# Two layer norms of a decoder layer: GpSimd's share moved to VectorE, the last sums taken by TensorE, and weight splits placed inside the first norm

## The reference, cut to what matters

```
def merge_and_ffn(x, oa, ob, ga, gb, w_oa, w_ob, w_out, ln1_g, ln1_b, w_ffn_in, w_ffn_out, ln2_g, ln2_b):
    pa = oa @ w_oa
    pb = ob @ w_ob
    mix = (sigmoid(ga) * pa + sigmoid(gb) * pb) @ w_out
    h = layer_norm(ALPHA * x + mix, ln1_g, ln1_b)
    gate, up = split(h @ w_ffn_in, 2)
    f = (silu(gate) * up) @ w_ffn_out
    return layer_norm(ALPHA * h + f, ln2_g, ln2_b)

def layer_norm(x, g, b):
    mu = mean(x); var = mean((x - mu) ** 2)
    return (x - mu) * rsqrt(var + 1e-5) * g + b
```

## Time and profile before

| | us |
|---|---|
| median of 3 runs (lowest to highest) | 1821.79 (1819.96 to 1823.74) |
| span of the profiled execution | 1823.3 |
| PE busy in the span | 1747.2 (96%) |
| DVE busy | 995.4 (55%) |
| ACT busy | 725.3 (40%) |
| POOL busy | 156.4 (9%) |

### The profile page before, as it was taken

How to read it: one execution, slowest core, us unless ns; L and a number is a source line. 1 busy time by engine, 2 the same in 40 slices (tenths; PEclk the granted TensorE clock), 3 DMA queues, 4 the chain that set the end, 5 groups by cost and what they waited for, 6 DMA issues and landing times.

```text
span 1823.3 us, 32494 instructions
## 1 busy us (share of the span) xinstructions
PE 1747.2 (96%) x12451; PEld 1660.6 (91%) x12451; DVE 995.4 (55%) x1389; ACT 725.3 (40%) x1054; POOL 156.4 (9%) x257
## 2 busy tenths in 40 slices
PE   8999999998999998999959999999999999999995
PEld 7999999766989896999959999999999999999995
DVE  4457667554377575666664444444444444444546
ACT  4343443353433232334344544443333333333333
POOL 1012222323010100000050000000000000000001
PEclk9999999897999998999979999999999999999997
DMA  6579999668688887677837878876775555556541
GB/s 217 155 267 315 324 321 342 164 180 256 223 301 298 306 290 233 220 228 252 254 128 237 256 246 265 250 230 213 259 224 165 167 161 161 165 167 200 163 155 52
DMA packets 204717, 410.75 MB, mean 225 GB/s; under 512 B 12220, under 2 KB 105686, under 8 KB 200416
## 3 DMA queue, kind: packets, MB, share of 16 engines
q1 hardware_dynamic: 178384, 254.41, 43.7%
q10 hardware_dynamic: 7488, 91.33, 15.0%
q0 software_dynamic: 18768, 63.94, 10.8%
HBM read 403.47 MB, written 94.92 MB: 273 GB/s over the span
## 4 chain that ended last, share of the span: by engine, by line
PE 77%; DVE 8%; DMA 7%; issue 4%; ACT 2%; POOL 1%; DVEq 0%; SPq 0%; ACTq 0%
PE bank L1289 74%; DMA VST<-in_cache_b_dram 3%; PE bank L1292 3%; DMA raw<-in_w_in_dram 3%; DVE wlo L898 1%; DVE PV L1091 1%; DVE PV L1094 1%; POOL U L572 1%; ACT L859 1%; DVE U L1205 1%; DVE U L1195 1%; DVE VST L1082 1%; ACT whi L615 0%; DMA xs_s<-in_x_sample_dram 0%; DVE VST L1085 0%
## 5 line engine op out<-in xcount | busy, mean ns | idle before, releaser
L898 DVE TENSOR_TENSOR wlo<-raw,whi 128x1024 fp32r<-128x1024 f32 x473 | 576.1, 1226 | 646.9 <-ACT whi L615 646.3
L615 ACT ACTIVATE whi<-raw 128x1024 fp32r<-128x1024 f32 x473 | 498.2, 1060 | 837.6 <-PE bank L1289 611.0
L1289 PE MATMUL bank<-X1H,whi 128*128 128x288 f32 x1408 | 420.1, 298 | 17.6 <-DVE X1L L1212 11.7
L1289 PE MATMUL bank<-X1L,whi 128*128 128x288 f32 x1408 | 417.4, 296 | 0.0
L1289 PE MATMUL bank<-X1H,wlo 128*128 128x288 f32 x1408 | 415.8, 295 | 0.0
L1289 PE MATMUL bank<-XH,whi 128*128 128x288 f32 x1248 | 375.1, 301 | 0.7 <-issue 0.5
L1289 PE MATMUL bank<-XL,whi 128*128 128x288 f32 x1248 | 369.9, 296 | 0.0
L1289 PE MATMUL bank<-XH,wlo 128*128 128x288 f32 x1248 | 368.6, 295 | 0.0
L1289 PEld LDWEIGHTS bank<-X1H,whi 128*128 128x128 f32 x1408 | 265.7, 189 | 21.5 <-issue 16.8
L1289 PEld LDWEIGHTS bank<-X1H,wlo 128*128 128x128 f32 x1408 | 267.0, 190 | 0.0
L1289 PEld LDWEIGHTS bank<-X1L,whi 128*128 128x128 f32 x1408 | 266.1, 189 | 0.0
(11 more groups left out here) (234 smaller groups left out, 1789.7 us busy)
## 6 DMA issues: line engine op xcount, KB each, us to landing
raw<-in_w_ffn_in_dram SPq DMA_DIRECT2D x176, 512.0 KB, 3.6
raw<-in_w_in_dram SPq DMA_DIRECT2D x156, 512.0 KB, 6.0
out_dram<-in_cache_b_dram ACTq DMA_DIRECT2D x28, 2336.0 KB, 10.9
raw<-in_w_ffn_out_dram SPq DMA_DIRECT2D x88, 512.0 KB, 4.1
KST<-in_cache_b_dram POOLq DMA_DIRECT2D x32, 512.0 KB, 5.1
QST<-tok_scratch POOLq DMA_DIRECT2D x32, 512.0 KB, 6.6
VST<-in_cache_b_dram POOLq DMA_DIRECT2D x16, 1024.0 KB, 12.9
raw<-in_w_out_dram SPq DMA_DIRECT2D x32, 512.0 KB, 5.3
```

The costliest lines, as they stand in the source:

```text
L615: nc.scalar.activation(whi[s][:, :], raw[s][:, :], ACT.Copy).then_inc(hi_done, 1)
L898: nc.vector.tensor_tensor(wlo[s][:, :], raw[s][:, :], whi[s][:, :].bitcast(F32), ALU.subtract).then_inc(lo_done, 1)
L1289: return nc.tensor.matmul(out, lhsT, rhs, start=start, stop=stop, **kw)
```

## The change

It has five parts.

1. POOL does nothing in the norms any more. DVE centres all four quarters and makes all 16 tiles of `X1L`. ACT adds the bias to all 16 tiles of `U` in the first half's feed-forward out, not 8.
2. The last tile of `U` and its square no longer go into DVE's running sums. PE multiplies them by `ones` directly and accumulates, so a norm has four float32 products where it had two. ACT reads the square of the mean out ahead of the mean, and DVE makes the variance before it waits for the mean.
3. The last group of the output projection stands unrolled on DVE, and the last split in it comes after the sums. The transpose that brings gains and biases (`LNP`) is moved from norm 1 to the end of the attention stage.
4. The splits of the chunks 3 to 8 of the feed-forward are written inside norm 1, two behind each of the quarters 1, 2 and 3, on ACT and DVE. The first feed-forward group is thereby unrolled on these two engines, and their loop runs over groups 1 to 10.
5. Behind the sums of each norm PE makes 13 float32 products (`WARM_UP`) into a bank that nobody reads.

The core of the diff:

```
+WARM_UP = 13
 ...
@@ gpsimd
-            centre_rest(0)
-            for k in range(8, KT):
-                pool.wait_ge(x1h_done, k + 1)
-                nc.gpsimd.tensor_scalar(U[:, k, :], U[:, k, :], LNP[:, 1, k:k + 1], None, ALU.add).then_inc(b_added, 1)
-                pool.wait_ge(b_added, k - 7)
-                nc.gpsimd.tensor_tensor(X1L[:, k, :], U[:, k, :], X1H[:, k, :].bitcast(F32), ALU.subtract)\
-                    .then_inc(x1l_rest, 1)
-            centre_rest(1)
@@ scalar, norm
+                nc.scalar.activation(RS[:, :], bank[4][:, 0:T], ACT.Square).then_inc(mu_done, 1)
                 nc.scalar.activation(MU[:, :], bank[4][:, 0:T], ACT.Copy).then_inc(mu_done, 1)
-                nc.scalar.activation(RS[:, :], bank[4][:, 0:T], ACT.Square).then_inc(mu_done, 1)
 ...
+                        if k in (7, 11, 15):
+                            for c in (k - 7) // 2, (k - 7) // 2 + 1:
+                                split(PH_F1[0], 0, c)
@@ scalar and vector, ffn_in
-                    for k in range(8):
+                    for k in range(6 if half == 0 and known_below(i, 1) else 0, 8):
                         split(ph, i, k)
 ...
-                loop(act, PH_F1[half], ffn_in)
+                if half == 0:
+                    ffn_in(0)
+                with act.Fori(1 - half, 11) as i:
+                    ffn_in(i)
@@ scalar, feed-forward out
-                    if half == 0 and k < 8:
+                    if half == 0 and k < KT:
                         act.wait_ge(x1l_done, k + 1)
                         add_b(0, k)
@@ vector
-            loop(dve, PH_OUT, outp)
+            with dve.Fori(0, 3) as i:
+                outp(i)
+            outp(3)
+            split(PH_OUT, 3, 7)
 ...
-                scale(0)
-                if which == 0:
-                    low(0)
-                centre(1)
-                scale(1)
-                if which == 0:
-                    low(1)
-                scale(2)
-                scale(3)
+                for n in range(4):
+                    if n:
+                        centre(n)
+                    scale(n)
+                    if which == 0:
+                        low(n)
+                        if n:
+                            split(PH_F1[0], 0, 2 * n - 2)
+                            split(PH_F1[0], 0, 2 * n - 1)
@@ tensor, norm
-                pe.wait_ge(sum_done, 33 * (which + 1) - 1)
-                mm(bank[4][:, 0:T], ones[:, :], SUMS[:, 0, :], True, True).then_inc(sum_pe, 1)
-                pe.wait_ge(sum_done, 33 * (which + 1))
-                mm(bank[5][:, 0:T], ones[:, :], SUMS[:, 1, :], True, True).then_inc(sum_pe, 1)
+                u_made(pe, which, KT - 1)
+                mm(bank[4][:, 0:T], ones[:, :], U[:, KT - 1, :], True, False)
+                pe.wait_ge(sum_done, 31 * (which + 1) - 1)
+                mm(bank[4][:, 0:T], ones[:, :], SUMS[:, 0, :], False, True).then_inc(sum_pe, 1)
+                pe.wait_ge(sq_done, KT * (which + 1))
+                mm(bank[5][:, 0:T], ones[:, :], SQ[:, 3, :], True, False)
+                pe.wait_ge(sum_done, 31 * (which + 1))
+                mm(bank[5][:, 0:T], ones[:, :], SUMS[:, 1, :], False, True).then_inc(sum_pe, 1)
+                for _ in range(WARM_UP):
+                    mm(bank[6][:, 0:T], ones[:, :], SUMS[:, 0, :], True, True)
```

More of the change, by code:

```diff
@@ L313, in build @@
         mix_done, mh_done, ml_done = sem("mix_done"), sem("mh_done"), sem("ml_done")
[L314 to L317, removed]
+        ax_done, sq_done, sum_done, sum_pe, mu_done, cen_done, var_done, sd_done, nrm_done, y_done, x1h_done, x1l_done = (
+            sem("ax_done"), sem("sq_done"), sem("sum_done"), sem("sum_pe"), sem("mu_done"), sem("cen_done"), sem("var_done"),
+            sem("sd_done"), sem("nrm_done"), sem("y_done"), sem("x1h_done"), sem("x1l_done"))
         sg_done, hh_done, hl_done = sem("sg_done"), sem("hh_done"), sem("hl_done")
@@ L1115, in _ @@
             nc.vector.tensor_copy(OROW[:, :], bank[6][0:NS, :]).then_inc(orow_done, 1)
+            dve.wait_ge(setup_pe, 2)
+            nc.vector.tensor_copy(LNP[:, :, :], bank[7][:, 0:64].rearrange("p (a k) -> p a k", a=4))
             dve.wait_ge(os_ready, 1)
@@ L1159, in sums @@
                 u_made(dve, which, n)
-                dve.wait_ge(sum_done, 33 * which + 2 * n + 1)
+                dve.wait_ge(sum_done, 31 * which + 2 * n + 1)
                 nc.vector.tensor_tensor(SUMS[:, 0, :], SUMS[:, 0, :], one(U, n), ALU.add).then_inc(sum_done, 1)
@@ L1169, in outp @@
                 for k in range(8):
-                    split(PH_OUT, i, k)
+                    if not (k == 7 and isinstance(i, int)):
+                        split(PH_OUT, i, k)
                     m = k // 2
@@ L1186, in outp @@
                         sums(0, n - 1, m - 1)
-                sums(0, 4 * i + 3, 3)
-            loop(dve, PH_OUT, outp)
+                if not isinstance(i, int):
+                    sums(0, 4 * i + 3, 3)
+            with dve.Fori(0, 3) as i:
+                outp(i)
+            outp(3)
+            split(PH_OUT, 3, 7)
             def norm(which):
-                dve.wait_ge(mu_done, 2 * which + 1)
                 v = [U[:, 4 * n:4 * n + 4, :] for n in range(4)]
@@ L1198, in scale @@
                 def scale(n):
[L1200 to L1203, removed]
+                    dve.wait_ge(cen_done, 4 * which + n + 1)
                     for k in range(4 * n, 4 * n + 4):
@@ L1214, in low @@
                             .then_inc(x1l_done, 1)
-                dve.wait_ge(mu_done, 2 * which + 2)
+                dve.wait_ge(mu_done, 2 * which + 1)
                 dve.wait_ge(sum_pe, 2 * which + 2)
@@ L1220, in norm @@
                 nc.vector.tensor_scalar(VAR[:, :], VAR[:, :], 0.0, EPS, ALU.max, ALU.add).then_inc(var_done, 1)
+                dve.wait_ge(mu_done, 2 * which + 2)
                 centre(0)
@@ L1239, in norm @@
                         nc.vector.tensor_copy(YTS[:, k * P:k * P + P], b[0:NS, 256:384]).then_inc(yt_odd, 1)
-            dve.wait_ge(setup_pe, 2)
-            link(nc.vector.tensor_copy(LNP[:, :, :], bank[7][:, 0:64].rearrange("p (a k) -> p a k", a=4)))
             norm(0)
@@ L1262, in ffn_in @@
                                                 ALU.subtract).then_inc(hl_done, 1)
-                loop(dve, PH_F1[half], ffn_in)
+                if half == 0:
+                    ffn_in(0)
+                with dve.Fori(1 - half, 11) as i:
+                    ffn_in(i)
                 if half == 1:
@@ L1274, in _ @@
                             if half == 0 and m == 0:
-                                dve.wait_ge(*((y_done, n + 4) if n < 8 else (x1l_rest, n - 4)))
+                                dve.wait_ge(y_done, n + 4)
                             nc.vector.scalar_tensor_tensor(out=U[:, n, :], in0=U[:, n, :], scalar=ALPHA if half == 0 else 1.0,
@@ L1280, in _ @@
                                     sums(1, n - 1, m - 1)
-                                if m == 3:
+                                if m == 3 and j < 3:
                                     sums(1, n, m)
@@ L1575, in _ @@
             cached_values(DB - 1)
+            pe.wait_ge(ln_in, 64)
+            turn(bank[7][:, 0:64], lnrow[:, :], 64).then_inc(setup_pe, 1)
             pe.wait_ge(orow_done, 1)
@@ L1622, in ffn_in @@
                         if half == 0 and k % 2 == 0:
-                            pe.wait_ge(*((x1l_done, 2 * k + 4) if k < 4 else (x1l_rest, 2 * k - 4)))
+                            pe.wait_ge(x1l_done, 2 * k + 4)
                         chunk_products(PH_F1[half], i, k, 4 * (k // 2), X1H, X1L, 2 * (k % 2), k < 2, k >= 6,
@@ L1632, in _ @@
             for k in range(KT):
-                pe.wait_ge(y_done, 8 + k + 1)
+                pe.wait_ge(y_done, KT + k + 1)
                 if k >= 8:
```

2 lines of the change are left out of this document (removed).

## The result

The changed kernel took 1801.38 us by the median of 4 runs (1798.15 to 1805.48), the kernel before 1820.88 us in the same job (4 runs, 1819.46 to 1823.74): a ratio of 0.9884, 95% interval 0.9867 to 0.9902. The forecast of 1800.6 us came from 21.2 us of gain; the medians give 19.5. Two later jobs gave 1801.70 (6 runs; 1822.46 before, ratio 0.9889, 0.9871 to 0.9908) and 1799.81 (5 runs; 1824.68 before, ratio 0.9874, 0.9854 to 0.9895).

The account below looks back on a forecast made before the run. PE, busy 96% of the span, was taken to bound the kernel through waits and lowered clock. 15.3 + 4.9 + 1.8 - 0.8 = 21.2 us off the 1821.8 median gave 1800.6 us, range 1796 to 1807.

Parts of the forecast that it names:

- Start of norm 1: Norm 1 up to the feed-forward: variance 2.6 us earlier, epsilon 1.2, centring 2.4; PE starts the feed-forward 6.2 us earlier.
- The rest of norm 1: First feed-forward group: DVE blocks of 7.15 us, PE reaching chunk 6 at 941.1 instead of 956.42; 15.3 us including the start.
- The idle products: Norm 1, around the 13 products: no PE time, but gaps of 1.2 and 1.7 us may cost clock; 0.8 us, bounds 0 to 2.9.
- Table loads: First half's feed-forward loop without table loads: 10 x 0.43 us, plus 0.57 at the half's end; 4.9 us.
- rival of the cache copies: First half's feed-forward: the 0.43 us per group comes from cache copies, so 4.9 us vanish, 1805.5; chance 0.06.
- Norm 2 and the stores: End of kernel: scaling 4.5 us earlier, first store 1.8 us earlier, then DMA sets the end; 1.8 us, bounds 0.5 to 3.
- At nothing: Moved LNP transpose and ACT's eight extra bias adds stand in waits, worth nothing; uncovered, under 0.5 us and 4 us.
- POOL is what slowed DVE: Norms; the rival denied this: POOL did not slow DVE, 3.6 us stay in each norm, 1809.8; chance 0.05.
- The clock was not low when the sums came: Norm 1; the rival said it was low, 17 products of 1.0 us holding PE up until 928.7, 1806.6; chance 0.08.
- The slower case: First feed-forward group: clock stays low throughout, chunks of 5.8 us, 5.3 us more, 1827; chance 0.03.
- clock term of 0: Around norm 1's idle products: by the Trainium skill such gaps lose no clock, giving 1799.7 us instead of 1800.6.

Follow-up runs that it names:

- e9: e7 with ACT's root ahead of the projection's last split and norm 2's last four squares, copies behind second and third scalings; 1798.08 us, changed kernel 1799.81.
- e5: Changed kernel with DVE adding the last tile's sum and square again, two TensorE products per norm; first feed-forward product 12.87 us behind the projection's last product, against 11.55.
- e4: Kernel before with one edit: ACT's first feed-forward group of the first half stands ahead of the loop, cache copies kept; 1819.85 us against 1823.23.
- e1_no_idle: Changed kernel without its 13 idle products (WARM_UP 0); one time, 1798.06 us; projection's last product to feed-forward group 1 takes 2.59 us longer.
- e7: Changed kernel plus 12 idle products at each half transition and, in norm 2, copies of tiles 1 and 3 ahead of the fourth scaling; tail 0.3 us shorter.
- e2: Changed kernel plus two useless 128x1152 subtractions on POOL in each norm; first feed-forward product 13.75 us behind the projection's last product, against 11.55.

## Why the prediction was right, point by point

- **Start of norm 1**, 6.2 us forecast, 18.07 - 11.55 = 6.52 measured: the variance 2.71 earlier (2.6 forecast), epsilon and centring 1.40 + 2.41 (1.2 + 2.4; the 1.2 should have been 1.3, which is 1.71 - 0.4). Not foreseen: what the step of the sums stands on. I had the square of the mean, behind the table load, as the last to be ready. e9 shows that the four products are as late, and e5 that the sums' way is worth 1.33 us of the 2.71; the other 1.38 fit the last split's place.
- **The rest of norm 1.** DVE's block measures 7.10 us (7.15 forecast). PE gets to chunk 6 at 936.08, 30.84 behind M (30.8 forecast), and the X1L that it needs ends at 935.58; no wait, with a slack of 0.5 us that the working gave as 0.4. Up to chunk 6 that is 15.54 us (15.3 forecast, less 0.8 for the clock), up to G 15.57. Undone singly, the splits cost 7.57, POOL's absence 3.55, the idle products 2.59, the sums 1.33, and the first group alone gave 1.82 to the kernel before. They add up to 16.9, more than 15.57. Each of the first four contains lost clock (1.7, 1.35, 2.59 and 1.0 us), and what is at half clock can be lost only once; that would explain the difference, but no run undoes two of them together.
- **The idle products.** The 0.8 us set aside for lost clock were not needed: the gaps of 1.16 and 1.59 us cost no clock, the granted clock is 1.00 from 907 on. The Trainium skill ("TensorE: Matmul & The Clock Gate", Why this matters for your kernels) warns only of longer gaps; by it the term was 0, and in norm 1 of the changed kernel that came out. Gaps of this size are not safe even so: at the transitions gaps of 1.87 to 1.90 us were followed by half clock in 12 of 17 cases, and the wait of 2.45 us in norm 1 of e5_sums_by_dve ended at half clock. The bound of 2.9 us for what is at stake was near: 2.59.
- **Table loads**, 4.9 us forecast, 4.41 measured. The rival of the cache copies is out: in e4 the copies stay and the 25.60 us are there. The term was mis-sized by a count: behind G lie nine steps from group to group, not ten. On PE they became 3.73 us shorter together, and the last group with the wait at its end 0.68. What e4 gave ahead of G, 1.82 us, is part of the 15.57.
- **Norm 2 and the stores**, 1.8 forecast, 1.93 measured; the variance comes 0.58 us earlier against Z (0.5 forecast), the first store 1.9 (21.9 before, 20.0 after; 1.8 forecast). DMA does set the end: in e1_no_idle the last big store is issued 0.85 us earlier against Z than in after (24.12 and 24.97), and the end comes no earlier (28.57 and 28.54). In e7 and e9 the last copy ends 1.5 and 1.4 us earlier, and the tail is 0.3 and at most 0.95 shorter. That it costs DVE's copies to wait behind all scalings was seen and is worth about 0.3 to 0.9 us.
- **At nothing**: H to Z is 567.04 before and 567.05 after, so ACT's eight bias adds cost nothing. The moved LNP transpose lies ahead of M, where its cost can't be read. That the half clock would move from one transition to the other I did not see. Before and after happen to have one such stretch each: that they cancel is luck, worth 1.5 us either way.
- **Rivals.** POOL is what slowed DVE (e2). The clock was not low when the sums came; in e5, with the longer wait, it was, so the condition of that rival was nearer than its 0.08 suggests. It cost 1.3 us there (F 12.87 against 11.55), not the 6.6 of the rival, since the clock was back at 909.0, with idle products queued up to 914.8. The slower case did not come near: the longest stretch of products at half clock in norm 1 in any variant of the changed kernel, in e1, is 5.8 us.
- **The sum.** 21.9 us behind M against 21.2. Two terms missed in opposite senses, the clock by 0.8 and the table loads by 0.5. The three jobs' medians give 19.5, 20.8 and 24.9; M spreads more than that in the profiles, and the range of 1796 to 1807 did not name it but covered it. So the forecast time is right by its terms, and that it lies within 1 us of the median is luck. The 1799.7 given for a clock term of 0 should read 1799.8.

## What to carry to other kernels

Compare two profiles from landmark to landmark, not by their spans: here the stages that no edit touched moved by up to 9 us, and the one time of e1_no_idle, taken by itself, would have thrown away products that are worth 2.6 us. Where TensorE waits ahead of a long run of products, count what the lost clock costs besides the wait (here 1.5 us at a transition, 2.6 in norm 1), and fill the gap with products that need nothing. When two things end together, such as the table load and the sums here, moving one of them alone is worth next to nothing: in e9_best it was 0.06 us.

## What the runs showed of the hardware

- **VectorE and GpSimd take whole turns.** In before, POOL's two centrings end at 916.00 + 2.60 = 918.60 (the row below; the earlier trace rows has the two in one) and at 921.24; DVE's epsilon ends at 918.77, and its centring, ready at 918.69, at 922.45, which is POOL's end plus 1.21, its own length nearly. In e2_pool_adds POOL's first ends at 917.07 and epsilon at 917.24, again 0.17 later; there DVE's centring began within 0.01 us of POOL's second instruction, ran at its 1.34, and POOL took 3.83: the 2.60 to 2.67 that the same form took in before, and most of the centring. The subtraction with an input in PSUM (VAR, 0.46 us at 916.57 in before) and the reciprocal (1.94 us at 918.43 in e2_pool_adds) were not held up beside POOL. The Trainium skill ("SBUF — State Buffer", SBUF: two separate sides) calls it "an exclusive lock, not a bandwidth split"; these rows agree. In the three cases with clearly different starts, epsilon twice and the centring of before, the one that started second paid; in the fourth the starts are too close to say which was first.

```profile
916.00 2.60 POOL L566 TENSOR_TENSOR U<-U,MU 128x1152 f32<-128x1152 f32 x1 [226.25 <-ACT MU L821]
```

- **The clock after a wait of under 2 us is not certain.** The same 1.87 to 1.90 us at the same place gave half clock in 12 of 17 cases and full clock in five, though the same in all three profiles of the changed kernel. A longer wait, 2.46 us at H of before, was followed by full clock. A stretch costs 1.5 us. Twelve idle products in the wait took it away six times out of six. What decides in the single case stays open.
- **Two table loads of 1.28 us in each group**, one ahead of the sigmoids and one behind the cache copy, cost PE only 0.43 us a group.
